# First root behind the products, two key levels moved to GpSimd, the output gate copied out raw

## What is computed

```python
def rmsnorm(x, g):
    return x * rsqrt(mean(x * x, axis=-1) + EPS) * g

def even_mixer(h, w_in, ...):              # h = rmsnorm(x, g0)
    hq, hf, hi, hgate, rq, rk, rv, rgate = split(h @ w_in)
    f = lb + (1 - lb) * sigmoid(hf)
    o_hg = scan(q=silu(hq), k=1 - f, logf=log(f), v=hi)      # chunks of 64
    o_ret = retention(rope(rq), rope(rk) * 128 ** -0.5, rv)
    ...

def scan(...):                             # per head, b = cumsum(log f)
    scores[t, s] = sum_d q[t, d] * k[s, d] * exp(b[t, d] - b[s, d])   # s <= t
    ...

def odd_mixer(h, w_in, ...):               # q, k, v, og from h @ w_in
    y = sigmoid(og) * head_rmsnorm(mlstm(q, k, v, gates))
```

## Time and profile before

| | |
|---|---|
| median of three runs | 955.35 us |
| the profiled execution's own time | 956.03 us |
| its span | 954.2 us |
| PE busy | 946.0 us, 99% |
| DVE busy | 702.2 us, 74% |
| ACT busy | 542.2 us, 57% |
| GpSimd busy | 52.6 us, 6% |
| granted TensorE clock, mean | 0.999 |
| moved by DMA | 187.26 MB, 196 GB/s |

### The profile page before, as it was taken

How to read it: one execution, slowest core, us unless ns; L and a number is a source line. 1 busy time by engine, 2 the same in 40 slices (tenths; PEclk the granted TensorE clock), 3 DMA queues, 4 the chain that set the end, 5 groups by cost and what they waited for, 6 DMA issues and landing times.

```text
span 954.2 us, 12826 instructions
## 1 busy us (share of the span) xinstructions
PE 946.0 (99%) x5052; PEld 817.8 (86%) x5052; DVE 702.2 (74%) x953; ACT 542.2 (57%) x733; POOL 52.6 (6%) x31
## 2 busy tenths in 40 slices
PE   9999999999999999999999999999999999999997
PEld 8898888888888889978888888888888888888886
DVE  6999556687888868996687888869546888755464
ACT  7855563765554557665765554558445657535433
POOL 0000000000000001030000000000000000003000
PEclk9999999999999999999999999999999999999999
DMA  9954436467767764434567777873765444566511
GB/s 328 311 182 136 173 133 195 136 223 260 246 225 243 253 213 164 146 133 137 194 223 260 244 226 244 289 211 126 232 213 180 150 160 148 165 217 237 203 45 45
DMA packets 122863, 187.26 MB, mean 196 GB/s; under 512 B 5331, under 2 KB 88756, under 8 KB 122804
## 3 DMA queue, kind: packets, MB, share of 16 engines
q1 hardware_dynamic: 122368, 186.05, 59.5%
q10 hardware_dynamic: 436, 0.40, 0.1%
HBM read 185.37 MB, written 1.06 MB: 195 GB/s over the span
## 4 chain that ended last, share of the span: by engine, by line
PE 95%; DVE 3%; ACT 1%; issue 0%; ACTq 0%
PE bank L692 93%; DVE arena L1232 1%; DVE wl L1226 1%; PE bank L941 1%; PE bank L1026 0%; ACT arena L1872 0%; DVE arena L1229 0%; DVE arena L1226 0%; PE bank L1105 0%; ACT L1872 0%; ACT wh L1877 0%; PE bank L893 0%; PE bank L752 0%; PE bank L950 0%; ACT sd L1872 0%
## 5 line engine op out<-in xcount | busy, mean ns | idle before, releaser
L1226 DVE TENSOR_TENSOR wl<-raw,wh 128x2048 fp32r<-128x2048 f32 (+1 forms) x157 | 359.6, 2293 | 128.9 <-ACT wh L1877 101.9
L1877 ACT CAST wh<-raw 128x2048 fp32r<-128x2048 f32 x155 | 294.9, 1912 | 125.6 <-PE bank L692 123.6
L692 PE MATMUL bank<-hx,wh 128*128 128x512 f32 (+1 forms) x1280 | 282.3, 360 | 0.1
L692 PEld LDWEIGHTS bank<-hx,wh 128*128 128x128 f32 x1280 | 224.0, 189 | 34.2 <-issue 0.7
L692 PE MATMUL bank<-wh,hx 128*128 128x512 f32 x560 | 179.7, 394 | 0.8 <-ACT hx L1872 0.5
L692 PE MATMUL bank<-hx,wl 128*128 128x256 f32 x1088 | 163.9, 284 | 0.0
L692 PE MATMUL bank<-wh,yh 128*128 128x512 f32 (+1 forms) x420 | 163.1, 388 | 0.0
L692 PE MATMUL bank<-wh,yl 128*128 128x512 f32 (+1 forms) x420 | 162.6, 387 | 0.0
L692 PE MATMUL bank<-wl,yh 128*128 128x512 f32 (+1 forms) x420 | 162.6, 387 | 0.0
L692 PEld LDWEIGHTS bank<-hx,wl 128*128 128x128 f32 x1088 | 146.7, 191 | 2.4
L692 PEld LDWEIGHTS bank<-wh,hx 128*128 128x128 f32 x560 | 104.8, 188 | 23.3 <-issue 1.6
(11 more groups left out here) (202 smaller groups left out, 711.9 us busy)
## 6 DMA issues: line engine op xcount, KB each, us to landing
raw<-in_mlp_w SPq DMA_DIRECT2D x64, 1024.0 KB, 5.3
raw<-in_w_in SPq DMA_DIRECT2D x40, 1024.0 KB, 5.1
raw<-in_ev_w_in SPq DMA_DIRECT2D x19, 1024.0 KB, 5.6
raw<-in_w_ada SPq DMA_DIRECT2D x12, 1024.0 KB, 5.1
raw<-in_od_w_in SPq DMA_DIRECT2D x12, 1024.0 KB, 5.2
raw<-in_ev_w_out SPq DMA_DIRECT2D x6, 1024.0 KB, 4.9
raw<-in_od_w_out SPq DMA_DIRECT2D x4, 1024.0 KB, 4.9
raw<-in_w_o_conv SPq DMA_DIRECT2D x4, 1024.0 KB, 5.0
```

The source lines that it names most:

```text
L692: return eng.matmul(o, l, r, start=start, stop=stop, skip_group_check=True)
L1226: return eng.tensor_tensor(o, x, y, op)
L1877: eng.copy(part(wh, u), part(raw, u)).then_inc(S["hi"], 1)
```

## The change

1. The first root. x is transposed as it is. `hh` and `hl` of the first norm hold x times gain, without the root. The outputs of the hf and hq units are multiplied by the root of each token on DVE (`h_scaled`, a row `x_row0` spread over the partitions by two small products, `root_spread`), the cosine and sine tables are multiplied by it once, and the hi, rv, hgate and rgate outputs get it as the scale of ACT's copy (`rs`). hi's second half, whose tokens stand in reverse, takes its own column (`root_back`). `idle_products` are 4 and none. Unit 0's weights land in four pieces, unit 1's in two, and `a_first` goes by quarters; unit 2 joins `LOW_LAST`.
2. The levels. The width 1 and the diagonal leave the items: seven are left (widths 64 to 2 and the blocks of 128), each one unit later in the list than an item of the same place before. GpSimd multiplies k by the next token's f, then by q (width 1), and q by k (diagonal), once the fourth item's `z` is done, sums the three tiles over the partitions, and DVE picks them from there (`row_picks`, in unit rgate 1). DVE's cumulative sum waits for GpSimd's first product, which reads f.
3. The odd mixer. `ML_SCORES` is (2, 3, 7, 4) and head 3 waits for nothing more. `t_evac` of mv 3's first half runs before the last `Silu`. mog 1's two halves are copied out raw, the first ahead of the root, and the sigmoid is taken in place later.

```diff
-ML_SCORES = (2, 3, 7, 2)
+ML_SCORES = (2, 3, 7, 4)
-LOW_LAST = (1, at("aq"))
+LOW_LAST = (1, 2, at("aq"))
...
-        ITEM_UNITS = [at("hi", 1) + n for n, c in enumerate((1, 1, 0, 1, 0, 1, 1, 1, 1, 2, 1)) for _ in range(c)]
+        ITEM_UNITS = [at("hi", 1) + n for n, c in enumerate((0, 1, 0, 1, 0, 1, 1, 1, 1, 1)) for _ in range(c)]
...
+                if u < 2:
+                    for n, landed in enumerate(pieces_landed(u)):
+                        c = piece_of(u, n)
+                        eng.dma_start(slot(raw, u)[:, c, :], unit_src(u)[:, c, :]).then_inc(landed, 16)
...
             eng.wait_ge(S["const"], 1)
-            idle_products(8)
-            eng.wait_ge(S["d_rows"], 32)
-            eng.transpose(PS[2][:, 0:ROWS1], rows1[0:ROWS1, :], ident[0:ROWS1, 0:ROWS1]).then_inc(S["colsT"], 1)
-            idle_products(3)
+            idle_products(4)
+            eng.wait_ge(S["d_ident"], 16)
             x_turn_first()
...
+            def root_spread():
+                eng.wait_ge(S["x_rs0"], 2)
+                for t in range(TT):
+                    m = mm(PS[7][:, tokens(t)], rs[:, t:t + 1].broadcast_to([P, P]), ident[:, :], True, True)
+                m.then_inc(S["x_bc0"], 1)
...
             def prenorm_first():      # VectorE
-                for t in range(TT):
-                    link(x_root(0, t))
-                    ts(work_t[:, t, :], x[:, t, :], rs[:, t:t + 1], None, ALU.mult).then_inc(S["x_w"], 1)
...
+                for n in range(4):
+                    split_piece(n)
+                    eng.wait_ge(S["hh"], 2 * n + 2)
+                    for k in (2 * n, 2 * n + 1):
                         stt(hl[:, k, :], x_bank(k), gain(0, k), hh[:, k, :].bitcast(F32), ALU.mult,
                             ALU.subtract).then_inc(S["hl"], 1)
+                x_root(0, 0).then_inc(S["x_rs0"], 1)
+            def h_scaled(u):
+                role, i = UNITS[u][4:]
+                wait_used(eng, u)
+                tt(g_qk[:, 2 * i:2 * i + 2, 1 if role == "hf" else 0, :], bank(u)[:, :].rearrange("p (h t) -> p h t", h=2),
+                   x_row0.unsqueeze(1).broadcast_to([P, 2, SEQ]), ALU.mult).then_inc(S["h_scaled"], 1)
...
+            def row_picks():
+                for half in range(2):
+                    eng.wait_ge(S["level_sum"], half + 1)
+                    eng.wait_ge(S["pred"], levels + half)
                     eng.copy_predicated(
...
+                        own_sum[:, half * 512:(half + 1) * 512].rearrange("p (n t) -> p n t", n=2)).then_inc(S["pred"], 1)
+                eng.wait_ge(S["level_sum"], 3)
+                eng.wait_ge(S["pred"], levels + 2)
+                pick_level(1, 6, next_sum)
...
             for u in range(-AHEAD, NU):      # VectorE
...
+                    eng.wait_ge(S["level_in"], 1)
                     for h in range(HEADS):
                         c = slice(h * SEQ, (h + 1) * SEQ)
                         m = eng.tensor_tensor_scan(g_b[:, c], reset, g_lf[:, c], 0.0, ALU.mult, ALU.add)
...
+                if u < 3 and u >= 0:
+                    h_scaled(u + 1)
                 for s in splits_at(u)[u in GROUP_AT:]:
...
+                if u == at("rgate", 1):
+                    row_picks()
+                if u == -2:
+                    first_root_row()
+                    h_scaled(0)
+                if u == -1:
+                    root_back()
...
             def prenorm_first():      # ScalarE
-                for t in range(TT):
-                    eng.wait_ge((S["d_x0"], S["d_x1"])[t], 16)
-                    x_root(0, t)
-                high_half(0)
+                eng.wait_ge(S["d_x0"], 16)
+                x_root(0, 0)
                 eng.wait_ge(S["cols"], 1)
...
+                high_piece(1, 0)
+                high_piece(1, 1)
+                eng.wait_ge(S["d_x1"], 16)
+                x_root(0, 1)
...
                         act(m_qk[:, c, :], m_qk[:, c, :], ACT.Silu).then_inc(S["qk"], 1)
+                        if j == 2:
+                            t_evac(at("mv", 3), 0)
...
+                    t_evac(at("mog", 1), 0)
                     eng.wait_ge(S["mvar"], 1)
...
             # GpSimd
+            q, k = g_qk[:, :, 0, :], g_qk[:, :, 1, :]
+            eng.wait_ge(S["k_hg"], 1)
+            eng.tensor_tensor(following, k[:, :, 0:SEQ:2], f[:, :, 1:SEQ:2], ALU.mult).then_inc(S["level_in"], 1)
...
+            eng.wait_ge(S["z"], 4)
+            eng.wait_ge(S["level_in"], 1)
+            eng.tensor_tensor(following, following, q[:, :, 1:SEQ:2], ALU.mult).then_inc(S["level_in"], 1)
...
+            for half in range(2):
+                h = slice(2 * half, 2 * half + 2)
+                eng.tensor_tensor(own_in[half].rearrange("p (h t) -> p h t", h=2), q[:, h, :], k[:, h, :],
+                                  ALU.mult).then_inc(S["level_in"], 1)
+            for half in range(2):
...
+                eng.partition_all_reduce(own_sum[:, c], own_in[half], P, bass.bass_isa.ReduceOp.add).then_inc(S["level_sum"], 1)
...
+            eng.partition_all_reduce(next_sum, next_in, P, bass.bass_isa.ReduceOp.add).then_inc(S["level_sum"], 1)
```

More of the change, by code:

```diff
@@ L409, in build @@
         decayed = (scr1[:, 2:4, :].rearrange("p a b -> p (a b)"), decayed1[:, :])
-        items = [(0, lv) for lv in range(7)] + [(0, 7), (1, 7), (0, 8)]
+        levels = 7
+        own_in, own_sum = (view(9728, 512), view(10752, 512)), view(4096, 1024)
+        next_in, next_sum = wf[:, 1536:2048], view(9728, 512)
         def mod_part(i):
@@ L548, in wait_bank @@
         def wait_bank(eng, u, b):
-            if BEFORE[u, b] is not None:
+            if BEFORE[u, b] is None:
+                return
+            if UNITS[BEFORE[u, b][0]][4] in ("hf", "hq"):
+                eng.wait_ge(S["h_scaled"], BEFORE[u, b][0] + 1)
+            elif BEFORE[u, b][0] == at("mog", 1):
+                eng.wait_ge(S["og_raw"], b + 1)
+            else:
                 wait_evac(eng, *BEFORE[u, b])
@@ L970, in small_turn, with level_scores @@
                 mm(PS[3][0:ATT_HEADS, 0:SEQ], rel_in, onehot, True, True).then_inc(S["colsT"], 1)
[L972 to L976, removed]
-                eng.wait_ge(S["z"], lv + 1)
[L978 to L986, removed]
+            def level_scores(lv):
+                dst, z = PS[2 + lv % 2], z_at(lv)
+                if lv >= 2:
+                    eng.wait_ge(S["pred"], lv - 1)
+                eng.wait_ge(S["z"], lv + 1)
+                for h in range(HEADS):
+                    m = mm(dst[:, h * P:(h + 1) * P], z[:, h, 0:P], z[:, h, P:2 * P], True, True)
                 m.then_inc(S["smm"], 1)
             def gated_out():
-                eng.wait_ge(S["pred"], len(items))
+                eng.wait_ge(S["pred"], levels + 3)
                 for t in range(TT):
@@ L1121, in _ @@
                     continue
-                if kind != "C" and u != 0:
+                if kind != "C" and u > 1:
                     eng.wait_ge(S["hi"], SPLIT_OF[u] + 1)
@@ L1264, in x_root, with split_piece @@
                 return eng.reciprocal(rs[:, t:t + 1], sd[:, t:t + 1])
[L1266 to L1270, removed]
+            def split_piece(n):
+                c = slice(n * UELEMS // 4, (n + 1) * UELEMS // 4)
+                eng.wait_ge(pieces_landed(0)[n], 16)
+                if n == 0:
+                    tensor(part(wh, 0)[:, c], part(raw, 0)[:, c]).then_inc(S["hi_first"], 1)
+                    eng.wait_ge(S["hi_first"], 1)
+                elif n < 3:
+                    eng.wait_ge(S["hi_piece"], n)
+                else:
+                    eng.wait_ge(S["hi"], 1)
@@ L1281, in prenorm_first @@
[L1281 to L1285, removed]
+                eng.wait_ge(S["colsT"], 1)
+                tensor(col1[:, :], PS[2][:, 0:ROWS1]).then_inc(S["cols"], 1)
+                eng.wait_ge(S["cols"], 1)
+                for n in range(4):
+                    split_piece(n)
+                    eng.wait_ge(S["hh"], 2 * n + 2)
+                    for k in (2 * n, 2 * n + 1):
@@ L1383, in rope @@
                     eng.wait_ge(S["d_tables"], 16)
+                    turns = tables[:, 0:2 * SEQ].rearrange("p (c t) -> p c t", c=2)
+                    link(tt(turns, turns, both(x_row0), ALU.mult))
                 eng.wait_ge(S["swap"], 2 * j + 2)
@@ L2045, in t_evac @@
                         eng.wait_ge(S["d_u"], 16)
+                    if role == "rgate" and i == 3:
+                        eng.wait_ge(S["pred"], levels + 3)
                     if role == "mog" and i == 1:
@@ L2203, in _ @@
                 elif UNITS[u][0] == "T" and i % 2 == 1 and u not in SECOND:
-                    for t in range(u == at("hi", 1), TT):
+                    for t in range(u in (at("hi", 1), at("mv", 3), at("mog", 1)), TT):
                         t_evac(u, t)
+                    if u == at("mog", 1):
+                        for t in range(TT):
+                            eng.wait_ge(S["og_raw"], t + 1)
```

(2 more changed lines are left out.)

213 lines of the change are left out of this document (115 added, 98 removed).

## The result

| | before | after |
|---|---|---|
| median | 955.35 us | 959.59 us (959.05 to 960.95, 5 runs) |
| ratio | | 1.0047, 95% interval 1.0035 to 1.0059 |
| profiled execution, its span | 956.03, 954.2 us | 959.59, 957.6 us |
| granted TensorE clock, mean | 0.999 | 0.995 |

A forecast was written before the change was run, and what follows sets the result against it. PE's own work, busy 99% of the span, was taken to bound the kernel. Start -1.75, unit 5 +0.6, levels -2.67, GpSimd's effect +0.9 and odd mixer -1.14 summed to -4.06: 951.3 us from 955.35, range 949.5 to 953.8.

The forecast's parts named there:

- The start: Units 0 and 1: transposes need only x, so PE starts unit 0 at about 8.8 us; 1.75 us gained.
- the clock stays low: Rival, unit 0: PE at 1.2 GHz until about 13.9 us, unit 0 ends 2.3 later than forecast; 953.6 us, chance 0.13.
- Unit 5's rest: Before unit 5: DVE's chain up to unit 5's subtraction comes late for PE; 0.6 us lost, ends 0 and 1.5.
- The levels' 2.67: Scan levels: three items, width 1 and the diagonal's two, leave PE at 0.89 us each; 2.67 us gained.
- The odd mixer: From head 2's scores to unit mog 0: two waits, for head 0's product on DVE and ACT's copy, go; 1.14 us gained.
- what GpSimd does to DVE: Levels: GpSimd's products and sums slow DVE, so PE waits about 0.9 us for keys; ends 0 and 5.9.
- the 4.1: Slack in us of the tightest key product behind GpSimd's chain, at old width 1's place: z at 94.83, wanted at 98.95.
- the bound of 5.9: Upper end of PE's wait for keys in the levels: DVE loses at most 10 us, less 4.1 of slack.
- the lock, slower: Rival, last two levels' keys: DVE stands still for all 15.6 us of GpSimd, PE 10.7 late; 961.1 us, chance 0.05.
- The turning point: In the lock rival: the sign turns once DVE loses more than 9.1 us, 5.0 of gain and 4.1 of slack.

The follow-up runs named there:

- the later start: Changed kernel with GpSimd's chain of products and sums started behind the fifth `z` in place of the fourth: 952.13 us, ratio 0.9965.
- the earlier chain: Changed kernel with GpSimd's chain of products and sums started behind the third `z` in place of the fourth: 958.66 us, ratio 1.0034.
- the early sum: Changed kernel with one added GpSimd sum over partitions of 128 columns near the start: 960.62 us, ratio 1.0061.

## Why the prediction was wrong, step by step

**The start: right in the trace.** PE's first products of the changed kernel:

```profile
0.90 3.78 PE L698 MATMUL bank<-ones 128*128 128x256 f32 x8 [0.90 <-DVE eps L1390]
5.25 1.38 PE L968 MATMUL bank<-ident,x 128*128 128x128 f32 x8 [0.56 <-DMA ident<-in_tbl]
6.61 1.09 PE L968 MATMUL bank<-ident,x 128*128 128x128 f32 x8
...
7.94 0.71 PE L698 MATMUL bank<-hx,wh 128*128 128x256 f32 x4 [0.24 <-DVE wh L1285]
...
13.62 4.48 PE L698 MATMUL bank<-hx,wh 128*128 128x256 f32 x36
17.93 0.60 PE L698 MATMUL bank<-ident,rs 128*128 128x128 f32 x4
```

Unit 0 starts at 7.94 (forecast 8.8) and ends near 14.2, behind 4 of the 36 products from 13.62 on (forecast 14.8). `root_spread` has no wait and costs some 0.4 us. Unit 1 ends at 20.5, 2.5 us earlier than before; the forecast had 1.75. The granted clock rose near 5.8 and not at 7.1, so the transposes ran faster than I had priced: 8 take 1.38 and 1.09 us. The rival "the clock stays low" is out. What the start is worth in time is another matter: beside the old items it was 0.3 us, and no run has the start alone beside the new ones.

**Unit 5's rest: right in size, wrong in place.** The loss appears one unit earlier, at the second bank of unit 4, and PE waits for the scaled output of unit 3, not for the subtraction. It is 0.66 against the forecast's 0.6:

```profile
35.54 0.69 DVE L1240 TENSOR_TENSOR arena<-bank,arena 128x512 f32<-128x512 f32 x1
...
36.29 0.50 PE L698 MATMUL bank<-wh,h_back 128*128 128x512 f32 x1 [0.66 <-DVE arena L1240]
```

The first row is DVE's, the second PE's. Unit 5 ends 1.54 earlier than before, -1.15 was the forecast for both steps.

**The levels' 2.67: not contradicted.** Three items of 0.89 are gone from PE. No run shows their worth alone; the account below closes with it.

**The odd mixer: right.** From head 2's scores to mog 0 it is now 1.23 us in place of 2.46, a gain of 1.23 against 1.14 forecast; alone it measured 1.0.

```profile
416.15 1.47 PE L698 MATMUL bank<-arena 128*128 128x256 f32 x8
417.38 0.48 PE L698 MATMUL bank<-wh,hx 128*128 128x512 f32 x1
```

**The step that failed is the last one of the levels, "what GpSimd does to DVE", +0.9.** It measured +8.8 on the span: 3.9 for the keys, 3.1 for ACT's wait, each with what PE loses in starting again, and 1.8 of clock. (-1.54 - 2.67 + 8.8 - 1.2 = +3.4, from 954.2 to 957.6. The medians differ by 4.2, as the profiled execution of the kernel before lies 0.7 above its median.) That DVE lost 8.8 too is chance: of its loss 4.9 were slack, and the rest of PE's came from ACT and the clock. The step failed three times.

1. *The count of what hits before the tight keys.* I let two sums and about 1 us of the products hit, 5.1 us. All three products and all three sums did. The price per sum, 2.05, was right twice (4.33 where 2.28 is usual, 3.40 where 1.35 is). But DVE was 3.0 late from the products, 1.7 more from the first sum and 2.05 more from the second, and so its keys, which without these 6.8 us would have started near 90.2, beside the first sum, started at 96.91, in the third. With that DVE lost 8.8, and PE waited 3.8. The slack was a little larger than the 4.1 that I took from the item in that place before: 8.8 of loss and 3.9 of delay leave 4.9. The delay was inside the bound of 5.9 that I had written; I chose the low side on the timing of each meeting in the trace of before, where DVE was not late.

2. *The second wait.* I followed the keys and not ACT's queue. The exp of the last level stands ahead of rv 3's evacuations, and those free rgate 0's banks. I asked what else is queued behind a late result for DVE and for PE, and not for ACT. The order alone, changed, gives 3.1 us (956.44), some of it by a shorter stretch at 1.2 GHz.

3. *The clock.* The rival that let it stay low was put at the start. The clock fell at 101.5, behind the gap of 3.8, and 1.8 us came on top of the two waits. The second gap isn't needed for it: with ACT's wait gone it fell all the same, for 3.5 us.

The rival "the lock, slower" named this place and this sign, and its 961.1 is 1.5 off. Its mechanism isn't what happened: it needs a DVE standing still for 15.6 us, and DVE lost 8.8. A two-input subtraction beside a sum took 4.33, 2.05 more than alone, while the shortest sum took 3.25. The Trainium skill, "SBUF — State Buffer", section "SBUF: two separate sides", has the engine that comes second blocked for the whole instruction; the rows agree with a conflict, and with less than the whole of it. The time came near 961.1 by luck: the rival took too much for the keys and left out ACT's queue and the clock, 4.9 us together.

The turning point it gave, a loss of DVE of 9.1, was too high, as it left out the same two. At 8.8 the kernel is already 4.2 us slower. With 3.0 lost (no sums) it gains 3.5.

That the loss of DVE was the cause is shown: without the sums, or with them behind the keys, the keys' wait and the stretch at 1.2 GHz are gone, and ACT's wait is 1.0 and 1.1 in place of 2.8. That ACT's order carried 3 us of it is shown by the run with the two banks emptied first. The 1.8 us of clock is read from the windows; no run changed the clock alone.

## What to carry to other kernels

When an engine B gets work that slows engine A, take the slack of every consumer of A behind that point, through the in-order queues of third engines too, and count the meetings on A's delayed timetable, not on the old one. Put such work behind the tightest consumer first; here one constant was worth 7.5 us, while the chain's own results were picked only at 116.21 us, 16 us behind its end. Two waits that hang on one late engine don't add up when removed singly: removing the first may show nothing.

## What the runs showed of the hardware

- GpSimd stands idle before a cross-partition sum that follows another kind of operation, with nothing it waits for: 5.64 us after the products, 5.71 with the later start, 7.21 with the earlier, 6.28 before the early sum and 5.98 once more in the same kernel. Right before each of these gaps the trace has two `MODIFY_POOL_CONFIG` on GpSimd's queue:

```profile
L2383 POOLq MODIFY_POOL_CONFIG  x2: 1/1/1, 83.7 to 83.7; - x2
```

In the changed kernel such a pair stands at 15.0 (from casts to products), 83.7 (from products to sums) and 606.4 us (from sums to products), at every change of kind and nowhere else. The kernel before has none between 17.0 and 603 us; so moving products and sums into the scan brought two changes of kind with it. The Trainium skill, "GPSIMD Engine Reference", section "Instruction dispatch", tells of about 6 us without a visible instruction at the first call into newly loaded code. The sizes agree; that it comes back after an earlier sum shows that it wasn't paid once here. The sums of the changed kernel, ready to go at 83.7, started 5.6 us later; whether they would have cost less without this, no run shows.

- A sum took 2.05 us from the DVE instructions beside it in several meetings, whatever they take alone: 0.68 became 2.73 in the kernel before, 2.28 became 4.33 and 1.35 (three products) 3.40 in the changed one. Others cost less: 1.7 for the first sum of the changed kernel, 0.2 for the first of the earlier chain. And DVE's eight products with one input from a PSUM bank, at 87.57 beside that first sum of the earlier chain, took 2.19 us, as they do with GpSimd idle (2.19 in the kernel without sums).
- A sum of 512 columns took 3.25 to 4.99 us. The first two of the changed kernel took 3.25 and 3.32 although DVE lost 1.7 and 2.05 beside them; the third, beside the three key products, took 4.35. So GpSimd pays too at times; none of the rows shown has such a sum with DVE idle beside it.
- In the profiles the clock rose at 3.7 to 10.0 us after the start of the span in kernels with the same start. Unit 0 then ended between 13.8 and 15.4, so a late rise costs at most 1.6 us, less than the 2.3 that the rival had. Why it varies isn't settled.
